# First attention of a two-block network: last head turns inside the last projection panel, first scores before the compressed keys, gates by exponential, compressed units alternating with window units

## The chip, the cores and the metric

One NeuronCore of a Trainium2 chip runs the whole program in one launch. The metric is the device time of that launch in microseconds (us). TensorE (PE) does matrix products and turns (transposes), VectorE (DVE) and ScalarE (ACT) the elementwise work, GpSimd (POOL) some small transfers, SyncE (SP) issues the weight transfers.

## The reference

256 tokens of width 1024 pass through two blocks of two layers each. The first block has a recurrent mixer (RWKV) with two convolution branches, a dense SwiGLU layer and a mixture of 8 experts. The second block has attention. The change lies in the first attention layer of the second block:

```python
q, kc, vc, ks, vs, kw, vw, q_mem, gl = jnp.split(h @ a_w_in[i], A_SPLITS, axis=-1)
o_main = nsa_attention(q, kc, vc, ks, vs, kw, vw, gl, ...)
o_mem = memory_attention(q_mem, mem_kv, mem_q_norm[layer], mem_k_norm[layer])
x = x + jnp.concatenate([o_main, o_mem], axis=-1) @ a_w_out[i]
x = x + squared_relu_mlp(rmsnorm(x, mlp_norm[layer]), w_up[layer], w_down[layer])
```

`nsa_attention` has 12 query heads over 3 key heads and three branches: compressed keys (15 blocks made by a small network with a GELU), selected keys and window keys. With 256 tokens, the selected and the window branch each are causal attention over all tokens. The three branch results are weighted by the sigmoid of the gates `gl` (36 columns) and added. `memory_attention` has 4 heads over 256 memory rows.

## The kernel before

The program is written engine by engine; the order on each engine is the order of its text, and engines meet only through semaphores. Weights come in panels of 128 x 2048 floats through a ring, and each product in full precision is made of three in split precision (high and low parts, `mm3`).

**Projection.** `attention_pe(0)` multiplies the tokens by panels 4 to 12 (`project_short`, `project_tokens`). Even panels go to bank 4, odd ones to bank 5, and each has two halves of 128 tokens. ScalarE copies a finished bank to `proj` (`panel`, L2218) and counts `attn_read`. VectorE normalises the heads set by set: `norm_squares` (L3210, L3212), then ScalarE's root (`head_std`, L2227), then `norm_turn` (from L3221 on), which counts `qk_ready`. TensorE turns the finished heads (`turn_heads`, L1504), ScalarE copies them to `qkT` (`turned_heads`, L2235, counts `turnq_act`). Panel 12 holds the memory queries (set 4) and the gates.

**Compressed keys.** `compress_hidden`, `compress_turned`, `compress_out` make them on TensorE; VectorE's `compress_keys` finishes them. TensorE's `compress_keys` then turns the keys (L1543, bank 7) and spreads the values with one product (L1544, bank 6); both are signalled by the fourth `cmp_mm`. ScalarE copies the keys to `cmp_kT` (L2341), VectorE the values to `cmp_v` (`compress_values`, L3297). TensorE's `compress_scores` (L1554) makes all compressed scores in banks 6 and 7; VectorE's `compress_scores` (L3309 to L3315) adds the mask and takes maxima, ScalarE exponentiates (`beside`, L2348), VectorE's `compress_weights` (L3322 to L3331) normalises and multiplies by the gates.

**Units.** The rest is a row of 14 units: one for each of 3 key heads and each kind for the second 128 tokens (`sel`, `cmp`, `win`), then 3 that hold both branches of the first 128 tokens (`both`), then 2 for the memory (`mem`). A full unit passes through: scores (PE, L1597 or L1590), mask and maxima (DVE, L3367 or L3361 to L3371), exponentials with sums (ACT, L2269 or L2264), turning of p (PE, L1624) and its copy (ACT, L2280), values (PE, L1638), finish (DVE, L3402 to L3429). A `cmp` unit has no scores, maxima or exponentials of its own, only turns (L1622), values and finish (L3396, L3397). The scores use two wide buffers in turn, the values banks 6 and 7 in turn (`bank[6 + u % 2]`).

The engines run these in a software pipeline with one step n for each unit. TensorE in step n: scores(n), transposed(n-2), with_values(n-3). ScalarE: exps(n), turned(n-1). VectorE: maxima(n), finish(n-4). What stands between them in step 1 to 3 are VectorE's `compress_scores`, the turn of set 4 and `compress_weights`; in step `LATE_TURN` = 4 TensorE turns item 9, the memory queries, into the bank that `TURN_BANK` gives, and ScalarE copies it in its step 3. `with_values(u)` waits for `finish(u-2)` (`pv_read`), `scores` of the q-th scored unit for the exponentials of the scored unit two before.

After the last unit come the turns of the output (`turn_o`), VectorE's split of the output weights (L3457, L3463) and of the turned output (L3508), and the output projection (L372 from 1659.78 us on).

## Time and profile before

| | |
|---|---|
| time, median of 3 runs | 2208.82 us |
| the runs | 2208.82, 2195.22, 2212.46 us |
| profiled execution, its own time | 2197.04 us |
| span of the profiled execution | 2195.2 us |
| TensorE products, busy | 2170.5 us, 99% |
| VectorE, busy | 1781.5 us, 81% |
| ScalarE, busy | 1072.0 us, 49% |
| mean granted TensorE clock | 0.997 |
| stretch of the first attention's units | about 1598 to 1660 us |

The page gives the busy time of an engine as a share of the whole span. The chain of waits follows the last instruction back to what released it at each step. The timeline shows instructions in order of time, those of one line merged; a bracket gives the idle time of the engine before them and what ended it.

### The profile page before, as it was taken

How to read it: one execution, taken by the hardware profiler on the slowest of the kernel's cores; microseconds unless marked ns; L12 is line 12 of the kernel's file. 1: busy time of each engine (PE TensorE's matmuls, PEld its weight loads, DVE VectorE, ACT ScalarE, POOL GpSimd, SP SyncE). 2: the span in 40 equal slices, each digit the busy share in tenths (PEclk: the TensorE clock that was granted, in tenths of full speed). 3: DMA queues.
4: the chain of work that ended last, by engine and by line, in shares of the span. 5: the costliest groups of instructions: out<-in, count | busy, mean ns of one | idle time of the engine just before them, and what ended most of it. 6: DMA issues, size and time to landing. Idle time of an engine off the chain costs nothing.

```text
span 2195.2 us, 40251 instructions
## 1 busy us (share of the span) xinstructions
PE 2170.5 (99%) x15594; PEld 1898.8 (86%) x15594; DVE 1781.5 (81%) x2161; ACT 1072.0 (49%) x1568; POOL 35.1 (2%) x44
## 2 busy tenths in 40 slices
PE   9999999999999999999999999999999999999999
PEld 8999899989999888888888888888888998877998
DVE  6886887778877789898988989898788777568777
ACT  6545400045366578787777878775473000342000
POOL 0000000000000000000000000000000000000000
PEclk9999999999999999999999999999999999999999
DMA  7333477643335799999999999995503555323554
GB/s 255 117 117 118 153 249 233 221 150 135 119 120 180 289 399 387 355 403 344 386 379 369 390 352 397 356 414 211 206 21 126 184 189 191 135 77 116 192 190 155
DMA packets 74117, 514.64 MB, mean 234 GB/s; under 512 B 8224, under 2 KB 8352, under 8 KB 14736
## 3 DMA queue, kind: packets, MB, share of 16 engines
q1 hardware_dynamic: 69552, 493.37, 59.8%
q0 software_dynamic: 4448, 19.59, 2.3%
q8 instruction: 88, 1.44, 0.3%
q14 instruction: 29, 0.24, 0.0%
HBM read 499.29 MB, written 13.63 MB: 234 GB/s over the span
## 4 chain that ended last, share of the span: by engine, by line
PE 87%; DVE 8%; DMA 2%; ACT 1%; issue 1%; SPq 0%; DVEq 0%; ACTq 0%
PE wide L372 30%; PE wide L1292 24%; PE wide L1291 24%; DMA ring<-in_weights 1%; DVE ring_lo L2472 1%; PE wide L1379 1%; PE wide L1638 1%; PE wide L1081 1%; PE wide L1089 1%; DMA ring_more<-in_weights 1%; PE wide L1624 1%; PE wide L869 0%; DVE ring_lo L3012 0%; PE wide L1504 0%; PE wide L1597 0%
## 5 line engine op out<-in xcount | busy, mean ns | idle before, releaser
L372 PE MATMUL wide<-ring_hi,hT_hi 128*128 128x512 f32 x664 | 262.3, 395 | 0.4 <-DVE ring_lo L3118 0.4
L1292 PE MATMUL wide<-ring_hi,hT_lo 128*128 128x512 f32 x664 | 262.1, 395 | 0.0
L2061 ACT ACTIVATE gate_s<-wide 128x512 f32<-128x512 f32 x43 | 25.8, 599 | 469.5 <-PE wide L1292 469.5
L3012 DVE TENSOR_TENSOR ring_more_lo<-ring_more,ring_hi 128x1024 fp32r<-128x1024 f32 x192 | 225.6, 1219 | 33.0 <-ACT ring_hi L2101 29.1
L372 PE MATMUL wide<-xT_hi,ring_hi 128*128 128x256 f32 x864 | 243.1, 281 | 1.1 <-DVE xT_lo L2460 1.0
L1292 PE MATMUL wide<-xT_hi,ring_lo 128*128 128x256 f32 x864 | 242.8, 281 | 0.0
L1291 PE MATMUL wide<-xT_lo,ring_hi 128*128 128x256 f32 x864 | 242.5, 281 | 0.0
L3012 DVE TENSOR_TENSOR ring_lo<-ring,ring_hi 128x1024 fp32r<-128x1024 f32 x192 | 226.3, 1220 | 18.6 <-ACT ring_hi L2101 16.0
L372 PE MATMUL wide<-mix_xT_hi,mix_hi 128*128 128x256 f32 x816 | 237.7, 291 | 0.8 <-DVE ring_lo L2472 0.7
L1292 PE MATMUL wide<-mix_xT_hi,ring_lo 128*128 128x256 f32 x832 | 233.4, 281 | 0.0
L1291 PE MATMUL wide<-xT_lo,mix_hi 128*128 128x256 f32 x816 | 229.3, 281 | 0.0
L2101 ACT ACTIVATE ring_hi<-ring_more 128x1024 fp32r<-128x1024 f32 x192 | 192.9, 1056 | 55.5 <-PE wide L372 48.6
L372 PE MATMUL wide<-ring_hi,xe_hi 128*128 128x512 f32 x544 | 219.9, 404 | 0.0
L3118 DVE TENSOR_TENSOR ring_lo<-ring,ring_hi 128x2048 fp32r<-128x2048 f32 x94 | 215.5, 2293 | 3.2
L1292 PE MATMUL wide<-ring_hi,xe_lo 128*128 128x512 f32 x544 | 214.4, 394 | 0.0
L1291 PE MATMUL wide<-ring_lo,hT_hi 128*128 128x512 f32 x536 | 210.2, 392 | 0.0
L2101 ACT ACTIVATE ring_hi<-ring 128x1024 fp32r<-128x1024 f32 x192 | 192.4, 1052 | 20.6 <-PE wide L372 16.7
L3116 DVE CAST ring_hi<-ring 128x2048 fp32r<-128x2048 f32 x93 | 114.1, 1227 | 104.7 <-DMA ring<-in_weights 104.6
L2472 DVE TENSOR_TENSOR ring_lo<-ring,mix_hi 128x1024 fp32r<-128x1024 f32 x120 | 141.5, 1220 | 39.4 <-ACT mix_hi L1834 38.2
L372 PEld LDWEIGHTS wide<-xT_hi,ring_hi 128*128 128x128 f32 x864 | 163.2, 189 | 4.0 <-issue 1.6
L1291 PEld LDWEIGHTS wide<-xT_lo,ring_hi 128*128 128x128 f32 x864 | 162.8, 188 | 1.6
L1292 PEld LDWEIGHTS wide<-xT_hi,ring_lo 128*128 128x128 f32 x864 | 162.5, 188 | 0.0
(557 smaller groups left out, 4794.0 us busy)
## 6 DMA issues: line engine op xcount, KB each, us to landing
ring<-in_weights SPq DMA_DIRECT2D x315, 1024.0 KB, 4.8
ring_more<-in_weights SPq DMA_DIRECT2D x120, 1024.0 KB, 6.3
xT<-in_weights SPq DMA_DIRECT2D x24, 1024.0 KB
routed_x<-xe_tm POOLq DMA_DIRECT2D x13, 512.0 KB, 7.0
ln_row<-in_ln_rows POOLq DMA_DIRECT2D x4, 1024.0 KB, 5.1
xe_tm<-routed_x SPq DMA_DIRECT2D x8, 512.0 KB
routed_x<-y_tm SPq DMA_DIRECT2D x7, 512.0 KB, 8.6
x_tm<-in_x SPq DMA_DIRECT2D x2, 512.0 KB, 4.8
```

Of the source, the lines that this page charges most:

```text
L372: ins = self.pe.matmul(out, lhsT, rhs, start=start, stop=stop)
L1081: ins = pe.matmul(o, lhs[hs, h, :], rhs[hs, h, :], start=True, stop=True)
L1089: straight = pe.matmul(bank[b][hs, h * CHUNK:(h + 1) * CHUNK], lhs[hs, h, :], chunk_ident[hs] if rhs is None else rhs[hs, h, :], start=Tru ...
L1291: pe.matmul(out, lhsT[0], rhs[1], start=False, stop=False)
L1292: return pe.matmul(out, lhsT[1], rhs[0], start=False, stop=stop)
L1379: ins = pe.transpose(bank[6 + s % 2][:, m * CAP:(m + 1) * CAP], h_tm[:, s % 2, m * P:(m + 1) * P], ident)
L2061: act.activation(gate_s[:, slot, :, :], b[:].rearrange("p (m t) -> p m t", m=2), func).then_inc(sems["out"], 1)
L2101: act.activation(panel_hi(k)[:, c], w[:, c], ACT.Copy).then_inc(S["panel_wide"], 1)
L2472: tt_(half_of(i, ring_lo[:, g % RING, :], half), half_of(i, ring[:, g % RING, :], half), half_of(i, mixer_hi[hi_slot(i)], half).bitcast(F3 ...
L3012: tt_(lo[:, c], w[:, c], panel_hi(k)[:, c].bitcast(F32), ALU.subtract).then_inc(S["panel_split"], 1)
L3116: copy(ring_hi[:, slot, :], ring[:, slot, :]).then_inc(S["split_hi"], 1)
L3118: tt_(ring_lo[:, slot, :], ring[:, slot, :], ring_hi[:, slot, :].bitcast(F32), ALU.subtract).then_inc(S["split"], 1)
```

## The change

- In the projection, the turns of items 6 to 11 (`turn_heads(0, 5, (3, 4, 5))`) stand between the two halves of panel 12 on TensorE, and ScalarE copies them (`turned_heads`) before it reads panel 12.
- TensorE turns the compressed keys and spreads the values in step 0 of the units, behind the first scores. The spread values go to bank 5 in place of bank 6, behind a wait for the read of panel 11. VectorE's `compress_values` moves from ahead of the squares of set 4 to step 0, behind maxima(0). The wait for `cmp_v` moves from the compressed scores to the first turned p.
- ScalarE does the root of set 4 and the gates ahead of the copy of the compressed keys. The gates are exp(-x) on ScalarE, and VectorE adds 1 and takes the reciprocal (`token_gates`) in step 1 behind its `compress_scores`. The wait for the gates moves there from `compress_weights` and from the first finish.
- The units of kind `cmp` and `win` alternate: sel, sel, sel, cmp, win, cmp, win, cmp, win. Through `scored`, this also moves the buffer of the late turn (`TURN_BANK`) and what it waits for.

```diff
@@ -626,7 +626,7 @@
         def units(l):
 
             if l == 0:
-                return [(kind, g, 1) for kind in ("sel", "cmp", "win") for g in range(NSA_G)] + [("both", g, 0) for g in range(NSA_G)] + \
+                return [("sel", g, 1) for g in range(NSA_G)] + [(kind, g, 1) for g in range(NSA_G) for kind in ("cmp", "win")] + [("both", g, 0) for g in range(NSA_G)] + \
                     [("mem", 0, tt) for tt in range(TT)]
             return [("two", s, 0) for s in range(SLOTS // 2)] + [("mem", 0, tt) for tt in range(TT)] + [("one", s, 1) for s in range(SLOTS)]
 
@@ -1479,13 +1479,15 @@
                     for tt in range(TT):
                         project_tile(n, tt, src, turn if n == n0 and tt == 0 else None)
 
-            def project_short(n):
+            def project_short(n, between=None):
 
                 j = SHORT.index(n - 4)
                 pe.wait_ge(S["attn_split"], j + 2)
                 w = in_panel(j)[2], ring_lo[:, panels.step(), :]
                 pe.wait_ge(S["attn_read"], n - 1)
                 for tt in range(TT):
+                    if tt and between:
+                        between()
                     for kb in range(KB):
                         ins = mm3(bank[4 + n % 2][:, tt * PC:(tt + 1) * PC], [t[:, kb, tt * P:(tt + 1) * P] for t in (in_hi, in_lo)],
                                   [t[:, kb * PC:(kb + 1) * PC] for t in w], start=(kb == 0), stop=(kb == KB - 1))
@@ -1541,13 +1543,13 @@
                 pe.wait_ge(S["cmp_k_ready"], 1)
                 for g in range(NSA_G):
                     pe.transpose(bank[7][:, g * 16:g * 16 + N_CMP], cmp_dup[0:N_CMP, g, :, :].rearrange("p d e -> p (d e)"), ident[0:N_CMP, 0:N_CMP])
-                pe.matmul(bank[6][0:NSA_R * N_CMP, 0:NSA_G * HEAD], atc[0:N_CMP, ATTN["cmp_spread"]], cmp_kv[0:N_CMP, 1, :, :].rearrange("p g e -> p (g e)"),
+                pe.wait_ge(S["attn_read"], 12)
+                pe.matmul(bank[5][0:NSA_R * N_CMP, 0:NSA_G * HEAD], atc[0:N_CMP, ATTN["cmp_spread"]], cmp_kv[0:N_CMP, 1, :, :].rearrange("p g e -> p (g e)"),
                           start=True, stop=True).then_inc(S["cmp_mm"], 1)
 
             def compress_scores():
 
                 pe.wait_ge(S["cmp_kT"], 1)
-                pe.wait_ge(S["cmp_v"], 1)
                 for h in range(NSA_HEADS):
                     hd = slice(HEAD * (h % 2), HEAD * (h % 2) + HEAD)
                     for tt in range(TT):
@@ -1612,6 +1614,7 @@
                     for j, e in enumerate(halves(u)):
                         if u == n0 and j == 0:
                             pe.wait_ge(S["attn_read"], sum(PANELS_ATTN[:l + 1]))
+                            pe.wait_ge(S["cmp_v"], 1)
                         if e >= 2:
                             pe.wait_ge(S["pT"], e - 1)
                         if l and u < n0 + 2 and 4 + e % 2 == TURN_BANK[1]:
@@ -1642,7 +1645,9 @@
                 for n in range(n_units + 3):
                     if n < n_units:
                         scores(n0 + n)
-                    if l == 0 and n == 1:
+                    if l == 0 and n == 0:
+                        compress_keys()
+                    elif l == 0 and n == 1:
                         compress_scores()
                     elif l and n == 1:
                         last_panel = sum(PANELS_ATTN) - 1
@@ -1681,9 +1686,7 @@
                     turn_heads(0, 4, (0, 1, 2))
                     project_short(11)
                     compress_out()
-                    project_short(12)
-                    turn_heads(0, 5, (3, 4, 5))
-                    compress_keys()
+                    project_short(12, lambda: turn_heads(0, 5, (3, 4, 5)))
                 else:
                     project_tokens(2, n_proj, turn=n_turn)
                     wait_xT(n_turn + 1)
@@ -2335,13 +2338,13 @@
                     act.activation(rs[0:N_CMP, 4:4 + NSA_G], rs[0:N_CMP, 4:4 + NSA_G], ACT.Sqrt, scale=1.0 / HEAD,
                                    bias=eps("rms_eps")[0:N_CMP]).then_inc(S["qk_std"], 1)
                     act.wait_ge(S["qk_std"], made.next("qk_std"))
+                    turned_heads((3, 4, 5))
                     panel(12)
-                    turned_heads((3, 4, 5))
+                    head_std(0, 4)
+                    act.activation(coef[:], proj[:, :, 2176:2212].rearrange("p t (h b) -> p b h t", b=3), ACT.Exp, scale=-1.0).then_inc(S["nsa_gates"], 1)
                     act.wait_ge(S["cmp_mm"], CMP_MM["kT"])
                     act.activation(cmp_kT[:, :, 0:N_CMP], bank[7][:, 0:NSA_G * 16].rearrange("p (g i) -> p g i", g=NSA_G)[:, :, 0:N_CMP],
                                    ACT.Copy).then_inc(S["cmp_kT"], 1)
-                    head_std(0, 4)
-                    act.activation(coef[:], proj[:, :, 2176:2212].rearrange("p t (h b) -> p b h t", b=3), ACT.Sigmoid).then_inc(S["nsa_gates"], 1)
 
                     def beside():
                         act.wait_ge(S["cmp_s"], 1)
@@ -3294,7 +3297,7 @@
                 own = atc[0:n, ATTN["cmp_own"]].unsqueeze(2).to_broadcast([n, NSA_R, HEAD])
                 dve.wait_ge(S["cmp_mm"], CMP_MM["kT"])
                 for g in range(NSA_G):
-                    ins = tt_(cmp_v[0:n, g, :, :], bank[6][0:n, g * HEAD:(g + 1) * HEAD].unsqueeze(1).to_broadcast([n, NSA_R, HEAD]), own, ALU.mult)
+                    ins = tt_(cmp_v[0:n, g, :, :], bank[5][0:n, g * HEAD:(g + 1) * HEAD].unsqueeze(1).to_broadcast([n, NSA_R, HEAD]), own, ALU.mult)
                 ins.then_inc(S["cmp_v"], 1)
 
             n_rows = NSA_HEADS * TT
@@ -3315,10 +3318,17 @@
                 tt_(s3, s3, cmp_mx.unsqueeze(2).to_broadcast([P, n_rows, N_CMP]), ALU.subtract).then_inc(S["cmp_s"], 1)
                 dve.wait_ge(S["cmp_s"], made.next("cmp_s"))
 
+            def token_gates():
+
+                dve.wait_ge(S["nsa_gates"], 1)
+                ts_(coef[:], coef[:], 1.0, None, ALU.add).then_inc(S["dve_step"], 1)
+                dve.wait_ge(S["dve_step"], made.next("dve_step"))
+                dve.reciprocal(coef[:], coef[:]).then_inc(S["dve_step"], 1)
+                dve.wait_ge(S["dve_step"], made.next("dve_step"))
+
             def compress_weights():
 
                 dve.wait_ge(S["cmp_e"], 1)
-                dve.wait_ge(S["nsa_gates"], 1)
                 dve.tensor_reduce(cmp_mx, s3, AX.X, ALU.add).then_inc(S["dve_step"], 1)
                 dve.wait_ge(S["dve_step"], made.next("dve_step"))
                 dve.reciprocal(cmp_mx, cmp_mx).then_inc(S["dve_step"], 1)
@@ -3406,8 +3416,6 @@
                         if kind in ("one", "two", "mem"):
                             ins = tt_(o, pv, inv_.unsqueeze(2).to_broadcast([P, k, HEAD]), ALU.mult)
                         else:
-                            if u == 0:
-                                dve.wait_ge(S["nsa_gates"], 1)
                             heads_ = slice(NSA_R * g, NSA_R * (g + 1))
                             if kind == "both":
                                 tt_(scale_.rearrange("p (b h) -> p b h", b=2), inv_.rearrange("p (b h) -> p b h", b=2), coef[:, 1:3, heads_, tile],
@@ -3435,8 +3443,11 @@
                         maxima(n0 + n)
                     if 1 <= n <= n_units:
                         sums(n0 + n - 1)
-                    if l == 0 and n == 1:
+                    if l == 0 and n == 0:
+                        compress_values()
+                    elif l == 0 and n == 1:
                         compress_scores()
+                        token_gates()
                     elif l == 0 and n == 2:
                         norm_turn(0, 4)
                     elif l == 0 and n == 3:
@@ -3488,7 +3499,6 @@
                     lower_short(7)
                     norm_turn(0, 3)
                     compress_keys()
-                    compress_values()
                     norm_squares(0, 4)
                 else:
                     copy_xT(n_turn, "kv_norm")
```

## Rows read from the trace of the kernel before

**Rows 1.** The page, busy time of each engine over the span.

```profile
PE 2170.5 (99%) x15594; PEld 1898.8 (86%) x15594; DVE 1781.5 (81%) x2161; ACT 1072.0 (49%) x1568; POOL 35.1 (2%) x44
```

**Rows 2.** The chain of waits, 1580 to 1700 us: start, length, engine, tile, line.

```profile
1603.24 1.28 ACT L2344
...
1604.87 1.28 ACT L2269
...
1620.86 1.09 PE wide L1597 x8
...
1631.52 1.73 PE wide L1638 x16
...
1659.78 0.47 PE wide L372
```

**Rows 3.** Timeline 1592 to 1606 us: start, length, engine, line, operation, times, [idle before].

```profile
1598.17 1.47 PE L1504 MATMUL wide<-cst,p_sb 128*128 128x128 f32 x12
...
1598.42 0.84 ACT L2218 ACTIVATE proj<-wide,rs 128x256 f32<-128x256 f32 x2 [2.90 <-PE wide L1292]
...
1599.85 0.53 PE L1544 MATMUL wide<-cmp_kv,atc 15*60 15x192 f32 x2
...
1600.49 1.08 DVE L3297 TENSOR_TENSOR cmp_v<-wide,atc 60x256 f32<-60x256 f32 x3 [2.59 <-PE wide L1544]
...
1600.89 0.21 ACT L2341 ACTIVATE cmp_kT<-wide 128x45 f32<-128x45 f32 x1
...
1600.91 2.00 PE L1597 MATMUL wide<-qkT 64*128 64x256 f32 x16 [0.53 <-ACT qkT L2235]
...
1601.49 0.67 DVE L3210 TENSOR_TENSOR scr<-proj 128x512 f32<-128x512 f32 x1
...
1602.75 2.85 PE L1554 MATMUL wide<-cmp_kT,qkT 64*128 64x15 f32 x48
...
1602.92 0.30 ACT L2227 ACTIVATE rs<-rs,cst 128x8 f32<-128x8 f32 x1 [1.82 <-DVE rs L3212]
```

**Rows 4.** Timeline 1606 to 1643 us, VectorE alone, in order of time.

```profile
1607.32 0.60 DVE L3309 TENSOR_TENSOR cmp_s<-wide,atc 128x180 f32<-128x180 f32 x2
...
1608.51 0.53 DVE L3315 TENSOR_TENSOR cmp_s<-cmp_s,rs 128x360 f32<-128x360 f32 x1
...
1612.54 0.20 DVE L3221 RECIPROCAL rs<-rs 128x8 f32<-128x8 f32 x1
...
1617.14 0.18 DVE L3402 RECIPROCAL rs<-rs 128x4 f32<-128x4 f32 x1
...
1622.04 0.70 DVE L3367 TENSOR_TENSOR wide<-wide,atc 128x512 f32<-128x512 f32 x1 [2.19 <-PE wide L1597]
...
1624.24 0.18 DVE L3402 RECIPROCAL rs<-rs 128x4 f32<-128x4 f32 x1
...
1625.10 0.70 DVE L3367 TENSOR_TENSOR wide<-wide,atc 128x512 f32<-128x512 f32 x1
...
1631.07 1.23 DVE L3361 TENSOR_TENSOR wide<-wide,atc 128x1024 f32<-128x1024 f32 x1
...
1637.54 0.18 DVE L3402 RECIPROCAL rs<-rs 128x4 f32<-128x4 f32 x1
...
1638.87 1.23 DVE L3361 TENSOR_TENSOR wide<-wide,atc 128x1024 f32<-128x1024 f32 x1
```

**Rows 5.** Windows: us, busy time of each engine, granted clock of TensorE (1.00 is full).

```profile
1605.60:1608.15 2.55, 0.00 (x0) 0.00 (x1) 2.41 (x6) 2.50 (x10) 0.00 (x0) 0.84 0.00 0
...
1608.00:1614.00 6.00, 5.85 (x26) 4.59 (x26) 4.49 (x8) 4.87 (x18) 0.00 (x0) 0.50 0.00 0
```

**Rows 6.** VectorE's groups by line and shape: count, busy us, mean ns.

```profile
L3324 DVE RECIPROCAL rs<-rs 128x24 f32<-128x24 f32 x1 | 0.3, 303 | 0.0
...
L2617 DVE RECIPROCAL norm<-norm 128x128 f32<-128x128 f32 x4 | 3.8, 953 | 3.4 <-ACT norm L1938 3.4
...
L2926 DVE TENSOR_SCALAR one_hot<-cst,moe_pos 128x128 f32<-128x128 f32 x2 | 0.5, 282 | 0.0
```

## The prediction

> **What bounds the kernel now.** Read the page's first part first: TensorE is busy for 99% of the span [rows 1], so a change pays only where TensorE waits or where a chain through the other engines is late. Then take the chain of waits for the stretch that the change touches, 1580 to 1700 us, and the timeline for the same stretch. Three places are to be seen there.
>
> The first is the start of the attention. Panel 12's products end at 1598.17, where the last turns start; those take until 1599.64 [rows 3]. ScalarE reads the panel, and only then copies the turned heads, so the first scores start at 1600.91, after 0.53 us of idle TensorE [rows 3]. ScalarE then waits for the squares, which stand on VectorE behind the compressed values; then come the root at 1602.92, a table load, the sigmoid, and a second table load at 1604.87 [rows 2, 3]. The third unit's scores need unit 0's exponentials. TensorE does nothing for 2.55 us, until 1608.15, and the granted clock falls in that gap and stays at 0.50 up to 1614 [rows 5].
>
> The second is the compressed run (units 3 to 5): VectorE waits 2.19 us until 1622.04 for the first window unit's scores [rows 4].
>
> The third is the rest: from unit 9 on, the spacing is set by ScalarE and TensorE together, and the last stretch up to 1659.78 [rows 2] by VectorE. The change alters no work there. So what counts is when VectorE starts unit 9's mask and maxima, now 1631.07 [rows 4].
>
> Behind the attention, nothing waits on a transfer: SyncE's ring issues wait for TensorE to release slots, and stay as they are relative to it. A shift of the attention's end is taken as a shift of the end of the kernel, one to one.
>
> **Part 1, turns inside panel 12, copies ahead of the panel's read.** No work is added. TensorE's 1.47 us of turns now stands between the halves of the panel, so the panel ends at 1599.64, and scores(0) start there, 1.27 us earlier than 1600.91; the copies ran under the second half. The price is that the panel's read starts at 1599.64 + 0.25 (now 0.25 after 1598.17) = 1599.9 and is over 0.87 later [rows 3], at 1600.8. The new wait in front of the second half needs set 3's heads, which VectorE has finished before it starts on the compressed keys; nothing stalls.
>
> **Part 2, keys and values behind the first scores.** TensorE: scores(0) 1.00 (half of the 2.00 for two units), the keys and the spread 0.74 (1599.64 to 1600.38), scores(1) 1.00 [rows 3]: 1602.4. The spread writes another bank, for which panel 11 was read long before. VectorE no longer does the values ahead of the squares: squares from 1600.8, the root 1.43 later (1601.49 to 1602.92 [rows 3]) at 1602.2.
>
> **Part 3, gates by exponential.** ScalarE: load 0.32 after the root begins (1602.92 to 1603.24), load and gate function 1.63 (1603.24 to 1604.87) [rows 2, 3]: 1604.15. I take the exponential to cost what the sigmoid did, same shape. The second load, 1.28, is gone. But the copy of the compressed keys, 0.21 [rows 3], was ahead of all this and is now behind it: done at 1604.4. **This is the wait that takes the place of the removed one**: TensorE has nothing from 1602.4 to 1604.4, then 2.85 us of compressed scores [rows 3], and scores(2) at 1607.3. Unit 0's exponentials (from 1604.4, 1.9 us as now between 1606.16 and 1608.15) are ready earlier. Against 1608.15 that is 0.85 gained, of 2.55 idle.
>
> The Trainium skill bears on this load: "ScalarE: Activation LUTs", section "What ACT_TABLE_LOAD costs", gives about 1.28 us for the load and another 1.38 for a drain, 2.66 together. Here a load takes 1.28 and the whole step with the gate function 1.63 [rows 2], so no such drain shows. With it, the keys would come 1.4 later and the total below would be larger by that; I go by the rows.
>
> On VectorE: maxima(0) 2.20 (1622.04 to 1624.24 [rows 4]) from 1602.2 to 1604.4; the compressed values 1.00 (1600.49 to 1601.49 [rows 3]) to 1605.4; maxima(1) to 1607.6; the compressed maxima 1.72 (1607.32 to the end of the 0.53 at 1608.51 [rows 4]) to 1609.3. Now the added pair, add and reciprocal of 72 elements. A reciprocal takes 0.30 at 24 elements and 0.95 at 128, an add at most the 0.28 of the 128 wide one [rows 6]. Ends: 0.45 and 1.2; on the line between them it is 0.60 + 0.25 with two gaps, 0.9. So 1610.2, and maxima(2) ends at 1612.4. That is 0.1 before the present 1612.54 [rows 4]. The head of the attention was to gain 1.3, and VectorE gives nearly all of it back.
>
> **Part 4, compressed and window units alternate.** Work is the same; the order of waits is not. In one step TensorE does scores(n), turns p of n-2, values of n-3; VectorE maxima(n), finish(n-4). The values of unit u use the bank that unit u-2 used, so they wait for finish(u-2), which on VectorE stands behind the maxima of the step before. In the present order that rarely bites, since the steps alike follow each other. Alternating, scores(6) are on TensorE, then little (a compressed unit), then values(4), which wait for finish(2), behind maxima(6), behind scores(6); and scores(8) stand behind values(4) in TensorE's queue. A loop through both engines, with no overlap between its halves:
>
> - the set's turn and the compressed weights 4.60 (1612.54 to 1617.14 [rows 4]): 1617.0; maxima(4) 2.20: 1619.2; finish(0) 0.86 (1624.24 to 1625.10 [rows 4]): 1620.1
> - values(2) 1.73 [rows 2], with the hand-over, 1621.85; scores(6) and hand-over 1.18 (1620.86 [rows 2] to 1622.04 [rows 4]): 1623.05; maxima(6): 1625.25; finish(2): 1626.1
> - values(4): 1627.9; scores(8): 1629.1; maxima(8): 1631.3; finish(4), now a window unit, 1.33 (1637.54 to 1638.87 [rows 4]): 1632.6, where unit 9's maxima start.
>
> Now 1631.07: **1.5 us later**. The moved turn of item 9 and its new bank lie beside this; it waits for exponentials that are long done, and its copy is off the loop. Removing the gate's wait in the finish and adding one for the compressed values ahead of the first turned p cost nothing: both are over by then (1605.4 against 1608.3).
>
> **The sum.** Head -0.1, alternation from there +1.6: +1.5 us, in a profiled execution of 2197.04 (span 2195.2, 1.8 around it): 2198.5.
>
> **The rivals.**
>
> *Slower, the clock falls again* (chance 0.33). TensorE is idle 2.0 us and then has only 15-column products for 2.85; now it is the products first and then 2.55 idle, and the clock fell [rows 5]. The order differs, the length hardly does. From when it decides: if the granted clock is 0.50 in any part of 1604 to 1609. Price: if it falls as the compressed scores start, these take up to 2.85 longer, which puts the compressed maxima at 1610.1 instead of 1607.6, +2.5; if it falls behind them, VectorE's own queue covers it, 0. Middle 1.2: total +2.7, between +1.5 and +4.0; 2199.7 for the profiled execution, 2206 at the level named below. In the Trainium skill, "TensorE: Matmul & The Clock Gate", section "What's actually happening", says that the throttled state is the default and activity releases it; by that the two cases look alike, which is why this has a third of the chance.
>
> *Faster, alternation spreads VectorE's load* (0.18). If the loop does not close, VectorE never waits from 1612.4 on: 4.60, three maxima 6.60, four short finishes 3.44, one long 1.33, sum 15.97, unit 9 at 1628.4: -2.7 us; 2194.3 for the profiled execution, 2201 at the level below. For it: the wait of 2.19 in the present order [rows 4] is real. Against: the order of TensorE's queue is fixed, as written above.
>
> *The spared load is not spared* (0.03): a load still stands before the first exponentials, 1.28. They then end at 1607.6, scores(2) move by 0.3, and VectorE's queue covers that: +1.5 all the same.
>
> *The forecast as summed*: 0.42. The remaining 0.04 is a disturbance over 1% in either direction.
>
> **Numbers.** All cases lie within 4 us of 2200, 0.2%; a measurement of this kernel tells about 1% from nothing. The level is less sure than the change: the three runs are 2195.22, 2208.82 and 2212.46, and the profiled one 2197.04, so their mean is 2203.4, and with +1.5, 2205. That is 3.8 below the shown median, which stands on two of the higher draws. The range takes in the single draws' scatter, from the lowest less the faster rival (2192.5) to the highest plus the slower one (2215.2), 2193 to 2215. Faster by over 1%: 0.03; within: 0.94; slower by over 1%: 0.03.
>
> **What would show it.** In the changed kernel: scores(0) about 1.3 earlier than now; one table load, not two, between the root and the first exponentials; TensorE idle about 2 us before the compressed scores, ended by ScalarE's copy of the keys; VectorE waiting about 2.2 us for scores twice in the window units, where it waited once; the values of units 2 and 4 waiting 1 to 2 us for VectorE's finish. The prediction is wrong if unit 9's maxima come sooner behind the start of panel 12's products than now, or if a second clock fall makes TensorE slow over the window units.

## The result, and the profile after

The changed kernel is slower by half a per cent: median 2213.93 us against 2196.78, 20 executions each; the ratio is 1.005 with a 95% interval of 1.0029 to 1.007. The three executions shown ahead of the prediction, two of them near 2210, were not typical: with the 140 that were measured beside the experiments, the kernel before has 160, with a median of 2197.3 and a mean of 2200.9.

Executions of both kernels fall into two groups, and the median jumps between them; nothing below can be read without that. In the upper group the mean granted clock is 0.992 or less. Before: 54 of 160 executions are in it, mean 2209.9, the others mean 2196.4. Changed (two sets of runs, 20 and 12): 19 of 32, mean 2217.5, the others mean 2200.4. So three things moved: the lower group by 4.0 us, the upper by 7.6, and the share of the upper one from 34% to 59%. With the old share, the first two make 0.66 x 4.0 + 0.34 x 7.6 = 5.2 us of the mean; the share makes the rest, 0.256 x 17.1 = 4.4; together the 9.7 by which the means differ (up to rounding). The share is the least certain of the three: the kernel before, in the five sets in which it was timed, had from 4 of 20 to 17 of 35 in the upper group.

The page of the changed kernel's profiled execution, which is one of the upper group:

```profile
span 2217.1 us, 40252 instructions
...
PE 2192.6 (99%) x15594; PEld 1916.8 (86%) x15594; DVE 1781.8 (80%) x2163; ACT 1071.0 (48%) x1567; POOL 35.2 (2%) x44
...
PEclk9999999999999999999999999999999999978999
```

TensorE is as busy in share as it was [rows 1], in a span 22 us longer: its busy time grew by 22.1 us without an instruction more. The clock row shows a 7 and an 8 near the end, where it had only nines before.

The head of the first attention in the timeline, changed kernel, to be read beside [rows 3, 4]:

```profile
1591.79 0.39 PE L372 MATMUL wide<-pT_sb_lo,o_tm_lo 128*128 128x256 f32 x1
...
1598.96 1.14 PE L1599 MATMUL wide<-qkT 64*128 64x256 f32 x8
...
1599.12 0.84 ACT L2221 ACTIVATE proj<-wide,rs 128x256 f32<-128x256 f32 x2 [2.12 <-issue]
...
1601.89 1.28 ACT L2344 ACT_TABLE_LOAD   x1
...
1603.18 0.31 ACT L2344 ACTIVATE coef<-proj 128x72 f32<-128x72 f32 x1
...
1603.40 0.19 ACT L2346 ACTIVATE cmp_kT<-wide 128x45 f32<-128x45 f32 x1
...
1603.64 4.75 PE L1556 MATMUL wide<-cmp_kT,qkT 64*128 64x15 f32 x48 [1.73 <-ACT cmp_kT L2346]
...
1608.50 0.60 DVE L3312 TENSOR_TENSOR cmp_s<-wide,atc 128x180 f32<-128x180 f32 x2 [1.65 <-PE wide L1556]
...
1610.26 0.20 DVE L3324 TENSOR_SCALAR coef<-coef 128x72 f32<-128x72 f32 x1
...
1610.49 0.60 DVE L3326 RECIPROCAL coef<-coef 128x72 f32<-128x72 f32 x1
...
1613.32 0.20 DVE L3224 RECIPROCAL rs<-rs 128x8 f32<-128x8 f32 x1
```

The first line is the start of panel 12's products; times behind that point are what can be compared between executions. The first scores come 7.17 us behind it; before, it was 8.51 (1600.91 - 1592.40), so the turn inside the panel gives 1.34. One table load is gone; the other takes 1.28, and the gates' exponential starts 0.01 behind its end, so the drain of about 1.38 us that the Trainium skill adds to a load ("ScalarE: Activation LUTs", section "What ACT_TABLE_LOAD costs") shows here no more than before. The compressed scores wait 1.73 us for ScalarE's copy of the keys, as forecast (2.0), and start 11.85 behind panel 12 instead of 10.35. Then comes what was not in the sum: the 2.85 us of compressed scores [rows 3] take 4.75, and VectorE's compressed maxima (L3312) wait 1.65 us for them. In the forecast the scores were over at 1607.3 and VectorE came for them at 1607.6, 0.3 us of room. The added pair on VectorE takes 0.20 and 0.60. The set's turn (last line) starts 21.53 behind panel 12 (before 20.14, forecast 20.0): without the wait of 1.65 it would be 19.9.

The window units of the same timeline, VectorE and the values that wait:

```profile
1617.92 0.70 DVE L3377 TENSOR_TENSOR wide<-wide,atc 128x512 f32<-128x512 f32 x1
...
1620.52 0.42 DVE L3428 TENSOR_TENSOR o_tm<-wide,rs 128x256 f32<-128x256 f32 x1
...
1621.00 3.35 PE L1641 MATMUL wide<-proj,pT_sb 128*128 128x64 f32 x16 [1.51 <-DVE o_tm L3428]
...
1626.48 0.70 DVE L3377 TENSOR_TENSOR wide<-wide,atc 128x512 f32<-128x512 f32 x1 [4.66 <-PE wide L1599]
...
1632.74 0.70 DVE L3377 TENSOR_TENSOR wide<-wide,atc 128x512 f32<-128x512 f32 x1 [2.45 <-PE wide L1599]
...
1636.26 1.23 DVE L3371 TENSOR_TENSOR wide<-wide,atc 128x1024 f32<-128x1024 f32 x1
```

The loop is there as the prediction has it: the values of unit 2 wait 1.51 us for VectorE's finish (those of unit 4 do not wait visibly here, where TensorE is slow; in a profile at full clock below they wait 0.78); maxima wait for scores twice, 4.66 and 2.45 us, where it was once 2.19 [rows 4]. But values(2) take 3.35 instead of 1.9, and unit 9's mask and maxima (last line) start 44.47 behind panel 12; before it was 38.67 (1631.07 [rows 4] - 1592.40). Forecast was +1.5, measured is +5.8 in this execution.

The windows of the same trace (us, busy time of each engine, granted clock in the third column from the right):

```profile
1604.00:1608.00 4.00, 4.00 (x45) 4.00 (x44) 2.78 (x6) 2.69 (x13) 0.00 (x0) 0.54 0.00 0
...
1608.00:1612.00 4.00, 3.74 (x20) 2.77 (x20) 3.29 (x8) 2.00 (x7) 0.00 (x0) 0.61 0.00 0
...
1616.00:1620.00 4.00, 3.49 (x32) 3.21 (x30) 3.83 (x6) 2.37 (x4) 1.50 (x3) 1.00 0.00 0
...
1620.00:1624.00 4.00, 3.00 (x16) 3.00 (x16) 1.61 (x7) 2.31 (x9) 0.00 (x0) 0.67 0.00 0
...
1624.00:1628.00 4.00, 4.00 (x18) 2.92 (x17) 1.49 (x2) 0.51 (x1) 0.00 (x0) 0.50 0.00 0
...
1970.00:2000.00 30.00, 30.00 (x99) 23.47 (x99) 12.91 (x34) 7.86 (x17) 0.00 (x0) 0.50 0.00 0
```

The clock was at half three times: in the head, as before [rows 5] but 3 us sooner; in the window units, where it had been at 1.00; and in the second attention, from 15.7 to 60.1 us behind its first score. The second attention has the same instructions in both kernels, and takes 62.9 us from its first score to the output projection (1950.42 to 2013.30), against 45.1 before (1944.95 to 1990.08): 17.8 us.

### The profile page after: what moved, and what is told of

Its sections match the earlier page's. It is cut to its first block, busy times and chain, and to the rows that moved or that the text cites. A ratio compares the mean times of both kernels' runs of the same rounds, so it can differ in the third digit from the quotient of the medians.

```text
span 2217.1 us, 40252 instructions
## 1 busy us (share of the span) xinstructions
PE 2192.6 (99%) x15594; PEld 1916.8 (86%) x15594; DVE 1781.8 (80%) x2163; ACT 1071.0 (48%) x1567; POOL 35.2 (2%) x44
## 4 chain that ended last, share of the span: by engine, by line
PE 89%; DVE 7%; DMA 1%; ACT 1%; issue 1%; SPq 0%; DVEq 0%; ACTq 0%
PE wide L372 30%; PE wide L1292 24%; PE wide L1291 24%; DMA ring<-in_weights 1%; PE wide L1588 1%; DVE ring_lo L2475 1%; PE wide L1641 1%; PE wide L1379 1%; PE wide L1081 1%; PE wide L1089 1%; PE wide L1627 1%; PE wide L869 0%; DVE rs L3379 0%; PE wide L1506 0%; DVE ring_lo L3121 0%
## 5 line engine op out<-in xcount | busy, mean ns | idle before, releaser
L3015 DVE TENSOR_TENSOR ring_more_lo<-ring_more,ring_hi 128x1024 fp32r<-128x1024 f32 x192 | 225.5, 1218 | 32.6 <-ACT ring_hi L2104 28.7
L2104 ACT ACTIVATE ring_hi<-ring 128x1024 fp32r<-128x1024 f32 x192 | 192.4, 1052 | 21.2 <-PE wide L372 16.3
```

The costliest lines, as they stand in the source:

```text
L2104: act.activation(panel_hi(k)[:, c], w[:, c], ACT.Copy).then_inc(S["panel_wide"], 1)
L3015: tt_(lo[:, c], w[:, c], panel_hi(k)[:, c].bitcast(F32), ALU.subtract).then_inc(S["panel_split"], 1)
```

## The experiments

Each was timed in 12 executions beside the kernel before. "Unit 9" is the start of unit 9's mask and maxima in the profiled execution, behind the start of panel 12's products; before 38.67, changed 44.47. "Set's turn" is the start of VectorE's reciprocal for set 4 (L3221 before, L3224 changed), counted from the same point.

| kernel | set's turn, us | from there to unit 9 | unit 9, us | clock falls in window units | lower group, mean | in upper group |
|---|---|---|---|---|---|---|
| before | 20.14 | 18.53 | 38.67 | no | 2196.4 | 54 of 160 |
| changed (20) | 21.53 | 22.94 | 44.47 | yes | | 12 of 20 |
| changed, again | 20.69 | 21.37 | 42.06 | yes | 2200.4 (both) | 7 of 12 |
| old order of units | 20.76 | 17.85 | 38.61 | no | 2197.9 | 4 of 12 |
| alternation alone | 20.14 | 23.28 | 43.42 | yes | 2200.1 | 3 of 12 |
| keys first | 19.94 | 25.76 | 45.70 | yes | 2200.8 | 1 of 12 |
| window units filled | 21.00 | 20.80 | 41.80 | no | 2200.0 | 3 of 12 |
| old order and keys first | 19.93 | 17.85 | 37.78 | no | 2196.1 | 2 of 12 |
| the same, head filled | 19.94 | 17.85 | 37.79 | no | 2197.6 | 2 of 12 |
| the same, gates later | 19.92 | 17.72 | 37.64 | no | 2195.6 | 7 of 12 |
| before, 50 products | 20.14 | 18.11 | 38.25 | no | 2206.4 | 2 of 12 |
| before, 26 products | 20.14 | 18.10 | 38.24 | no | 2202.0 | 1 of 12 |
| changed, 8 products | 20.21, 21.18 | 20.64, 28.23 | 40.85, 49.41 | no, yes | 2202.5 (both) | 9 of 24 |
| changed, 16 products | 21.29, 20.51 | 28.46, 20.65 | 49.75, 41.16 | yes, no | 2204.2 (both) | 12 of 24 |
| changed, 24 products | 22.12 | 21.37 | 43.49 | yes | 2206.7 | 3 of 12 |
| changed, 32 products | 20.60 | 21.17 | 41.77 | yes | 2207.6 | 5 of 12 |

The second column splits the path: the set's turn on VectorE ends the head, and what follows up to unit 9 is the stretch of the loop. From unit 9 to the output projection all profiles but one take 28.7 us (one of those with 8 products 30.7), so what is lost at unit 9 is lost at the end. The three profiles of the kernel before have the same first attention and differ by 0.4 us at unit 9; a smaller difference between two profiles tells nothing.

The upper group is told by the mean clock of the whole execution, so it doesn't always mean a slow second attention. Four executions lie between the groups (clocks of 0.993 and 0.994, 2207.0 to 2210.6 us; one each of "head filled", of the two runs with 16 products and of the first with 8) and are counted in the lower one, which raises that group's mean for "head filled" from 2196.6 to 2197.6.

### Old order of the units

```diff
-return [("sel", g, 1) for g in range(NSA_G)] + [(kind, g, 1) for g in range(NSA_G) for kind in ("cmp", "win")] + ...
+return [(kind, g, 1) for kind in ("sel", "cmp", "win") for g in range(NSA_G)] + ...
```

> The changed kernel with the units back in their old order (three compressed, then three window units); all else as changed. Theory 1 (the loop through TensorE and VectorE that alternation closes costs 2 to 3 us in the first attention, more where the clock falls in it): unit 9's maxima come 2.5 us or more sooner behind panel 12 than in the changed kernel (44.5 us there), and the undisturbed executions, 2198 to 2204 in the changed kernel, lie at 2195 to 2197. Rival 1 (the lost time of the first attention is the wait for the compressed keys): unit 9's maxima move by under 1 us. On the second attention, where the changed kernel's profile has the clock at half for over 40 us: if only the shift in time matters, its executions are again spread over two groups 15 us apart, in shares that may be anything; if alternation itself is the cause, the upper group is as rare as before (4 of 20).

Median 2198.9, ratio 1.0003 (0.9975 to 1.0031). Panel 12's start and unit 9's maxima in its timeline:

```profile
1591.89 0.39 PE L372 MATMUL wide<-pT_sb_lo,o_tm_lo 128*128 128x256 f32 x1
...
1630.50 1.23 DVE L3371 TENSOR_TENSOR wide<-wide,atc 128x1024 f32<-128x1024 f32 x1
```

38.61 us apart: 5.9 less than in the changed kernel, and the same as before. The clock falls in the head here too, and not in the window units. Theory 1 holds, rival 1 falls. It also shows that the rest of the change is worth nothing that can be told: the first scores come sooner, but the compressed maxima wait 0.86 us for scores made at half clock, the set's turn starts 0.6 later than before, and the units behind it make that up. The lower group is 1 us above the expected band.

### Alternation alone

The kernel before with the same line changed the other way:

```diff
-return [(kind, g, 1) for kind in ("sel", "cmp", "win") for g in range(NSA_G)] + ...
+return [("sel", g, 1) for g in range(NSA_G)] + [(kind, g, 1) for g in range(NSA_G) for kind in ("cmp", "win")] + ...
```

> The kernel before with only the order of the units changed to alternate. Theory 1: unit 9's maxima come 2 to 4 us later behind panel 12 than before (38.7 us there), the lower group of executions at 2198 to 2200. Rival 1: within 1 us of before. For the second attention as for the run with the old order: a shift of 2 to 4 us may change how often the clock falls.

Median 2200.88, ratio 1.0006 (0.998 to 1.0032).

```profile
1591.36 0.19 PEld L372 LDWEIGHTS wide<-pT_sb_lo,o_tm_lo 128*128 128x128 f32 x1
...
1634.78 1.23 DVE L3361 TENSOR_TENSOR wide<-wide,atc 128x1024 f32<-128x1024 f32 x1 [0.74 <-PE wide L1597]
```

43.42 us, 4.75 more than before and over the expected 2 to 4; the lower group, 2200.1, is 3.7 above before. The head is as before (set's turn at 20.14 in both), so all of it lies behind the set's turn, where only the order of the units differs. So alternation by itself costs the lower group nearly all of what the whole change costs it (4.0). The ratio, over both groups, doesn't resolve this.

### The compressed keys first

```diff
 panel(12)
+act.wait_ge(S["cmp_mm"], CMP_MM["kT"])
+act.activation(cmp_kT[...], bank[7][...], ACT.Copy).then_inc(S["cmp_kT"], 1)
 head_std(0, 4)
 act.activation(coef[:], ..., ACT.Exp, scale=-1.0).then_inc(S["nsa_gates"], 1)
-act.wait_ge(S["cmp_mm"], CMP_MM["kT"])
-act.activation(cmp_kT[...], bank[7][...], ACT.Copy).then_inc(S["cmp_kT"], 1)
```

> The changed kernel with ScalarE's copy of the compressed keys put back ahead of the root and the gates, alternation kept. Theory 1: the compressed scores start about 2 us sooner and TensorE's wait of 1.7 us ahead of them goes, but VectorE sets maxima(2), so unit 9's maxima move by under 1 us unless the clock is kept at full, then by up to 3 us. Rival 1: unit 9's maxima come 1.7 us sooner or more at the same clock. Theory 2 expects the share of the upper group to change with any shift.

Median 2200.42, ratio 1.0007 (0.9985 to 1.0029). The compressed scores and unit 9's maxima; panel 12 starts at 1591.97:

```profile
1601.93 3.63 PE L1556 MATMUL wide<-cmp_kT,qkT 64*128 64x15 f32 x48
...
1637.67 1.23 DVE L3371 TENSOR_TENSOR wide<-wide,atc 128x1024 f32<-128x1024 f32 x1
```

TensorE's wait is gone, the scores start 9.96 behind panel 12 instead of 11.85, and unit 9 comes at 45.70, no sooner. But with the clock at half from about 1621 to 1634, this profile has the longest fall of the first three alternating kernels, and unit 9 alone can't tell what the wait cost. The set's turn can: it starts at 19.94 instead of 21.53, and the compressed maxima no longer wait, though the clock fell in the head here too. So the wait for the keys did cost the head 1.6 us in the changed kernel's profile, by leaving the slow compressed scores too late for VectorE. What it saved here was lost again in the window units, 25.76 against 22.94. Neither theory 1 nor rival 1 is settled by unit 9, since the clock was not the same; in the old order the repair is worth 0.8 (38.61 against 37.78, below).

### Both repairs, and two additions to them

Old order and keys first:

> Both repairs: the units in their old order, and the copy of the compressed keys ahead of the root and the gates; the rest as changed. Theory 1: the compressed scores at 10 us behind panel 12 (11.85 changed, 10.35 before), unit 9's maxima at 37.5 to 38.6 (before 38.7, old order alone 38.6), lower group at 2195 to 2197: no better than before, since VectorE's queue in the head (values, compressed maxima, gates) is as long. Rival: the head's gain of 1.3 us reaches the end, unit 9's maxima at 37.4 or less, lower group at 2194.

Median 2196.3, ratio 0.9999 (0.9977 to 1.002).

```profile
1593.17 0.19 PEld L372 LDWEIGHTS wide<-pT_sb_lo,o_tm_lo 128*128 128x128 f32 x1
...
1630.95 1.23 DVE L3371 TENSOR_TENSOR wide<-wide,atc 128x1024 f32<-128x1024 f32 x1
```

37.78 us: 0.9 sooner than the profile of before that was shown, 0.5 sooner than its two others. The lower group's mean is 0.3 below before, well inside the interval. Nothing that can be told from no change, though it undoes the loss.

Head filled, with products whose result nobody reads:

```diff
 elif l == 0 and n == 1:
+    pe.wait_ge(S["attn_read"], 13)
+    keep_busy(bank[4][:, 0:P], 4)
     compress_scores()
+    keep_busy(bank[4][:, 0:P], 4)
```

> The repaired kernel (old order of units, keys copied first) with four products of 0.21 us ahead of and four behind the compressed scores, to keep TensorE at work where the clock falls in every profile so far. Theory 3: the clock stays at 1.00 from 1600 to 1616 us; unit 9's maxima come 36.5 to 37.5 us behind panel 12 (37.78 without). Rival: the clock falls all the same, and the products, then 0.42 us each, put scores(2) later: unit 9's maxima at 38 to 40.

Median 2196.91, ratio 0.9978 (0.9952 to 1.0003). Windows:

```profile
1604.00:1608.00 4.00, 4.00 (x45) 3.48 (x44) 3.83 (x8) 2.69 (x13) 0.00 (x0) 1.00 0.00 0
...
1608.00:1612.00 4.00, 2.92 (x26) 2.57 (x25) 3.76 (x8) 2.69 (x8) 0.00 (x0) 1.00 0.02 4
...
1970.00:2000.00 30.00, 29.22 (x93) 22.26 (x93) 14.78 (x41) 8.64 (x19) 0.00 (x0) 0.50 0.00 1
```

The clock stays at 1.00 through the head, in this profile alone of all, and unit 9's maxima are at 37.79, unchanged from 37.78. Theory 3 is right on the clock and wrong on its worth in this kernel: with the keys first, the compressed maxima don't wait for TensorE even at half clock (the set's turn is at 19.93 without and 19.94 with the products), so VectorE's queue sets the head and the half clock hides under it. In the changed kernel it does not hide. There the scores start 1.9 us later, and in all eight profiles of the changed first attention (two above, six below) the maxima wait for them, from 0.31 us, where the clock fell 14.0 us behind panel 12, to 2.23, where it fell at 11.5; the mean is 1.12. The first with 8 products, and the one with 24:

```profile
1606.78 0.60 DVE L3312 TENSOR_TENSOR cmp_s<-wide,atc 128x180 f32<-128x180 f32 x2 [0.31 <-PE wide L1556]
...
1609.28 0.60 DVE L3312 TENSOR_TENSOR cmp_s<-wide,atc 128x180 f32<-128x180 f32 x2 [2.23 <-PE wide L1556]
```

The set's turn starts 19.9 behind panel 12 plus this wait in each of them. (The last line of the windows shows that the second attention of this very execution still ran at half: from 15.7 to 60.1 us behind its first score, exactly as in the changed kernel's two profiles, though this kernel has the old order.)

Gates later on VectorE:

```diff
 elif l == 0 and n == 1:
     compress_scores()
-    token_gates()
 elif l == 0 and n == 2:
+    token_gates()
     norm_turn(0, 4)
```

> The repaired kernel with the add and the reciprocal of the gates behind maxima(2) instead of ahead of them on VectorE. Theory 1 (in the head, VectorE's queue sets the third unit's exponentials): these come 0.85 us sooner, unit 9's maxima between 0 and 0.85 us sooner than 37.8 us behind panel 12; lower group at 2195. Rival: unchanged, since the set's turn and the compressed weights behind it are as late as they were.

Median 2207.42, ratio 1.0017 (0.999 to 1.0045), 7 of 12 in the upper group; unit 9 at 37.64, 0.14 sooner. The rival is right but for that tenth: what follows on VectorE is as late as it was. The lower group's 2195.6 is the lowest here, and yet the median is 10 us above before: how many executions fall in the upper group outweighs all else.

### The window units filled

```diff
 def transposed(u): ...
+    if l == 0 and kind == "cmp":
+        keep_busy(bank[4 + e % 2][:, 256:384], 5)
```

> The changed kernel with five products of 0.21 us, into a part of a bank that nobody reads, ahead of the turns of each compressed unit, where TensorE would else wait for VectorE's finish. Theory 3 (the window units run at half clock because TensorE waits in the loop): the granted clock stays at 1.00 from 1616 to 1636 us, and unit 9's maxima come at most 42 us behind panel 12, against 44.5. Rival 3 (the clock falls there for another reason, the products are only added work): the clock falls as before and unit 9's maxima come at 45 us or later.

Median 2200.84, ratio 1.0021 (0.9996 to 1.0047). Windows:

```profile
1616.00:1620.00 4.00, 4.00 (x37) 3.74 (x34) 3.77 (x7) 2.57 (x6) 0.55 (x1) 1.00 0.00 0
...
1620.00:1624.00 4.00, 3.95 (x33) 3.40 (x32) 1.49 (x6) 1.74 (x8) 0.00 (x0) 1.00 0.00 0
...
1624.00:1628.00 4.00, 4.00 (x32) 3.53 (x30) 2.88 (x7) 3.30 (x11) 0.00 (x0) 1.00 0.03 6
```

The clock is at 1.00 where the changed kernel had 0.67 and 0.50, TensorE's busy time is 3.95 to 4.00 of 4, and unit 9 comes at 41.80, under the bound of 42: theory 3 holds for this profile. One profile alone is thin, since in two of eight without the products the clock doesn't fall either; but in those two the clock fell latest in the head, 13.7 and 14.0 us behind panel 12, and here it fell at 13.1, between others (12.9 and 13.5) that did lose it again in the window units, which speaks for the products. The stretch behind the set's turn takes 20.80, against 22.94 in the changed kernel and 20.64 and 20.65 in the two where the clock happened to stay: the added products cost 0.15, and the rest of the distance to their 40.85 and 41.16 is the wait in the head (1.10 us here). The loop's own cost, at full clock, is 20.64 less 18.53: 2.1 us, or 2.5 by the two other profiles of before. The lower group's mean is only 0.4 below that of the changed kernel, so what the filling gains over 12 executions is not told from nothing.

### The changed kernel again

> The changed kernel, unaltered, beside the others on one chip. The longer delay changed the share of the upper group (over 2210 here, the one in which the second attention keeps a halved clock) to 2 of 12 and no other variant had more than 4 of 12, against 12 of 20 for the changed kernel. If that share is the changed kernel's own, 6 or more of 12 come out here and the median is 2210 or more; if it was the day's or the chip's, 1 to 5 of 12 and a median of 2200 to 2203.

Median 2214.44, ratio 1.0042 (1.0012 to 1.0073), 7 of 12 in the upper group, as expected if the share is the kernel's own. The kernel before had 9 of 35 beside it; in 12 executions that makes it likely, not certain. Unit 9's maxima, with panel 12 at 1591.08:

```profile
1633.14 1.23 DVE L3371 TENSOR_TENSOR wide<-wide,atc 128x1024 f32<-128x1024 f32 x1
```

42.06 us this time: the same program, 2.4 us less than in its first profile; the clock was at half in the window units for half as long (1.6 us of the difference), and the compressed maxima waited 0.79 us instead of 1.65.

### Delays ahead of the second attention

In `attention_pe(1)`; the last number is that of products into bank 7 that nobody reads:

```diff
-turn_x(n_turn, x_tm, lambda tt: pe.wait_ge(S["y_read_2"], tt + 1), (0, 1, 1))
+turn_x(n_turn, x_tm, lambda tt: pe.wait_ge(S["y_read_2"], tt + 1), (0, 1, 51))
```

First with the kernel before, 50 and 26 products more:

> The kernel before with 50 more 128x128 products into a bank that nobody reads, ahead of the second attention's projection: a delay of 5.4 us at most at full clock, nothing else changed. Theory 2 (the second attention loses the clock in more executions because it comes 4 to 6 us later, its own instructions being the same): the upper group, 4 of 20 executions before, becomes more than half; median about 2213 or higher. Rival 2 (chance, or something in the changed first attention): 4 of 20 stays, and the median is about 2202.

> The kernel before with 26 more products ahead of the second attention's projection. Each took 0.21 us of TensorE in the run with 50, where the shift was 10.3 us, so this shifts the second attention by about 5.4 us, as in the changed kernel's profile. Theory 2 in its weak form (the share of the upper group depends on the amount of the shift): half or more of 12 in the upper group. Rival 2 (it does not): 1 to 5 of 12, the lower group at 2201.

Medians 2206.47 (ratio 1.0037, 1.0014 to 1.006) and 2202.31 (1.0009, 0.9986 to 1.0032). The first was mis-sized by me: the 50 products shifted the second attention by 10.7 us and not 5.4 (from the first output projection to the second attention's first score 295.83 us, before 285.17; the 10.3 in the second expectation is a little low). The two lower groups are 10.0 and 5.6 above before: a shift does go to the end nearly one to one, as the prediction took it. Upper group 2 of 12 and 1 of 12: theory 2, that coming later is enough, has fallen.

Then with the changed kernel. Theory 4 said that not the amount but the place matters, relative to what the first attention leaves behind, and that the share would go down, up, down, up with 8, 16, 24, 32 products:

> The changed kernel with 8 more products of 0.21 us ahead of the second attention's projection, which shift the second attention by 1.7 us and change nothing else. So far 19 of 32 executions of the changed kernel lie in its upper group (2212 and more), and both its profiles have the clock fall 15.7 us behind the second attention's first score. Theory 4 (what the first attention does in the changed kernel sets at which moment, relative to the second attention's work, the clock is decided, and there the moment is the bad one): a shift this small takes it out of the bad place, 3 of 12 or fewer in the upper group. Rival 4 (something of the changed kernel other than the moment makes the second attention slow): 6 to 9 of 12 remain.

> The same with 16 products, a shift of 3.4 us. Theory 4: the share differs from that with 8 products, and may come back to more than half. Rival 4: 6 to 9 of 12 for both numbers. If both shifts give 3 of 12 or fewer, any shift removes it and the moment is only partly supported.

> The changed kernel with 8 products ahead of the second attention's projection, as in the run before with 8 (3 of 12 in the upper group). Theory 4 (the moment): again 4 of 12 or fewer. Rival 4 (the changed kernel's share is the same wherever the second attention lies, or all is chance): about the same share as with 16, 24 and 32 products.

> With 16 products, as in the run before with 16 (6 of 12). Theory 4: again 6 or more of 12. Rival 4: the same share as with 8 and 24.

> With 24 products, a shift of 5.1 us. Theory 4: 4 of 12 or fewer, as with 8. Rival 4: the same share as with 16 and 32.

> With 32 products, a shift of 6.8 us. Theory 4: 6 or more of 12, as with 16 and with none. Rival 4: the same share as with 8 and 24.

Medians 2202.86, 2212.61, 2206.84, 2212.17, 2207.21, 2210.08. In the upper group: none 19 of 32; 8 products 3 and 6 of 12; 16 products 6 and 6; 24 products 3; 32 products 5. The first half went as theory 4 expects; then 8 products gave 6 instead of at most 4, and 32 gave 5 instead of at least 6. Together 12 of 36 for 8 and 24, 36 of 68 for none, 16 and 32: the direction fits, but with shares of 33% and 53% in such numbers chance is not excluded. This stays open. One profile also shows what the mean clock hides: the second with 8 products is counted in the upper group (0.991, 2210.31 us), but its second attention takes an ordinary 47.1 us; it was its first attention that stayed long at half clock (unit 9 at 49.41).

What they showed more firmly is by the way. They hold the changed first attention six times more, so with the two profiles of the changed kernel there are eight of it: unit 9 at 44.47, 42.06, 40.85, 49.75, 49.41, 41.16, 43.49 and 41.77, mean 44.1. In six of eight the clock falls in the window units. In the seven profiles with the old order it never does. The windows of the one with 8 products in which it doesn't fall, and the values of units 2 and 4 there (third line: the second attention):

```profile
1620.00:1624.00 4.00, 4.00 (x31) 3.33 (x31) 1.60 (x3) 1.70 (x5) 0.00 (x0) 1.00 0.00 0
...
1624.00:1628.00 4.00, 3.22 (x25) 2.53 (x25) 2.11 (x7) 2.56 (x10) 0.00 (x0) 1.00 0.01 2
...
1970.00:2000.00 30.00, 27.11 (x137) 21.75 (x137) 22.19 (x55) 11.72 (x26) 0.00 (x0) 0.89 0.10 36
...
1619.29 2.00 PE L1641 MATMUL wide<-proj,pT_sb 128*128 128x64 f32 x16 [0.74 <-DVE o_tm L3428]
...
1625.55 2.00 PE L1641 MATMUL wide<-proj,pT_sb 128*128 128x64 f32 x16 [0.78 <-DVE o_tm L3428]
```

## Why the prediction went as it did

**The head** was right at full clock, and there only. The gain at the first scores (1.27 forecast, 1.34 measured), the new wait for the keys (2.0 and 1.73), the added pair (0.85 without gaps and 0.80), and VectorE's queue up to the set's turn (20.0 and 19.9 without waits) came as summed. But the sum left 0.3 us between the end of the compressed scores and VectorE's coming for them, and the clock fell in the head in all eight profiles of the changed first attention. The rival "slower, the clock falls again", given 0.33, came true by its own condition, and its middle price of 1.2 is near the mean wait of 1.12. It should have had the larger chance: the clock had fallen in the same place before. Only with the keys copied first does the fall in the head cost nothing (set's turn at 19.93 with it and 19.94 without).

**The loop** was right in kind and a little small. From the set's turn to unit 9 the forecast had 20.2 (1612.4 to 1632.6), and at full clock it is 20.64 and 20.65. Against before, forecast +1.6, measured +2.1.

**The step that failed** is the price of the loop's waits. "A loop through both engines, with no overlap between its halves" was costed at full clock throughout, and the clock rival was looked for in "any part of 1604 to 1609" only. A second fall "over the window units" is named as a sign of being wrong, but no term of the sum and no rival has a price for it. The loop makes TensorE idle in a stretch where it had been busy (before, 4.00 of 4 us in 1616 to 1620 and 1620 to 1624), and there the granted clock fell, in six of eight profiles and in both other alternating kernels without filling; in the one profile with products to fill the waits it stayed, and with the old order it stayed in all seven. At half clock TensorE's half of the loop takes up to twice the time (the scores of unit 6 took 2.08 us, against 1.13 in a profile at full clock; the values of unit 2 took 3.35, against 2.00), and VectorE waits for it: from the set's turn to unit 9 it took 21.2 to 28.5 us where the loop alone has 20.6. The mean of unit 9 over the eight is 44.1, +5.5 over before: +0.9 in the head, +2.1 for the loop, +2.5 for the half clock in the window units. The sum had -0.1, +1.6 and nothing, and the slower rival ended at +4.0. The 5.2 us that the two groups moved are near it. That the waits are what loses the clock is shown by the order of the units, both ways, and by one filled profile; why two of eight executions keep it is open.

**The second wrong step** is "A shift of the attention's end is taken as a shift of the end of the kernel, one to one". For an inserted delay it holds (10.0 and 5.6 in the lower group, for shifts of 10.7 and 5.3). For the changed kernel it doesn't: its second attention runs at half clock in more executions. In both of its own profiles the clock falls 15.7 us behind the second attention's first score and comes back 60.1 us behind it; in the profile of before it falls only 44.7 behind it, and briefly. The same fall, 15.7 to 60.1 behind, with the same 62.9 us, stands in the profile of the old order with the head filled: it is a state that other variants can enter too, and which the changed kernel entered more often (19 of 32 against 54 of 160). The larger share makes 4.4 us of the mean and the whole jump of the median. Why the share is 59% is not settled: not the shift alone (delays), not alternation alone (3 and 1 of 12), not the rest alone (4 of 12).

**The level**: 2205 was 3.8 below the median shown then and 8 above that of many executions, so the forecast time told nothing of the sign. That 2213.93 lies within 2193 to 2215 is luck: the range was made from three draws of two groups, and the measured median is one of the upper group. "Within 1%" is what came, but the text took all under 1% for nothing, where 20 executions tell 0.5% from none. "Faster, alternation spreads VectorE's load" was wrong as argued: the wait of 2.19 became two waits.

## What to carry to other kernels

When steps of unequal size alternate in a pipeline whose queues are fixed, write down for each wait which earlier step on the other engine it stands behind; equal steps in a run may overlap where alternating ones form a loop with no overlap. Where a sum leaves only some tenths between the end of one engine's work and another's coming for it, price it at half clock too: here 0.3 us of room became a wait of 1.1 on average. Price every new idle stretch of TensorE twice, once as idle time and once as the time in which its work behind that runs at half clock, wherever nothing hides TensorE, and not only where the clock fell before. With executions in two groups, compare groups and shares, and look in a trace at which stretch makes the group; a median of three tells of neither.

## What the runs showed of the hardware

- The same first attention took from 69.6 to 80.1 us from panel 12 to the output projection in eight executions of the same code, by where the clock fell (40.85 to 49.75 at unit 9). Before, three profiles lie within 67.0 to 67.4.
- The half clock can hold through a stretch in which TensorE is called busy all the time: 30.00 of 30 us at 0.50 in the second attention (1970 to 2000), while the same stretch of time, in the execution with 8 products at a mean clock of 0.89, has 27.11. In the window units the half clock held from under 4 to over 27 us, by execution.
- Products that nobody reads, in time that was idle anyway, went with a clock of 1.00 in the head (8 of 0.21 us; in all 17 other profiles it fell there) and in the window units (15 of 0.21 us; without them it fell in 8 of 10 alternating ones), in the profile of each.
- A plain product of 128x128 by 128 cost 0.21 us of TensorE, by the shift of 10.7 us for 50. The trace shows each as two instructions, a turn of the same size as one (104 for the 52 products there), and turns follow each other at 0.11: per instruction the cost is the same, though each is shown with a duration of 0.27.
